# An expert kernel in which TensorE's transposes of the activation move up by one half chunk, and one VectorE subtraction moves behind two others

## The reference, cut to what matters

```
def _clamped_swiglu(hgu):
    x_glu = jnp.minimum(hgu[..., ::2], SWIGLU_LIMIT)
    x_lin = jnp.clip(hgu[..., 1::2], -SWIGLU_LIMIT, SWIGLU_LIMIT)
    return x_glu * jax.nn.sigmoid(SWIGLU_ALPHA * x_glu) * (x_lin + 1.0)
...
    xs = h[tok]
    hgu = lax.ragged_dot(xs, w_gate_up, group_sizes) + b_gate_up[e_sorted]
    act = _clamped_swiglu(hgu)
    out = lax.ragged_dot(act, w_down, group_sizes) + b_down[e_sorted]
    out = out * gates.reshape(-1)[order][:, None]
    return jax.ops.segment_sum(out, tok, num_segments=L)
```

## Time and profile before

| what | value |
|---|---|
| median of 3 runs | 1986.39 us (1986.01 to 1989.12) |
| the profiled execution's own time | 1986.01 us |
| its span, first to last instruction | 1984.3 us |
| mean granted TensorE clock | 0.984 |
| TensorE matmul busy | 1932.5 us (97%) |
| VectorE busy | 1703.8 us (86%) |
| ScalarE busy | 1372.4 us (69%) |
| GpSimd busy | 471.1 us (24%) |

### The profile page before, as it was taken

One profiled execution on the slowest core, in us unless ns is written; L12 is line 12 of the kernel. 1 busy time (PEld: TensorE's weight loads), 2 busy tenths in 40 slices (PEclk: granted clock), 3 DMA queues, 4 the chain that ended last, 5 costly groups with the idle time before them and its releaser, 6 DMA issues.

```text
span 1984.3 us, 29677 instructions
## 1 busy us (share of the span) xinstructions
PE 1932.5 (97%) x8812; PEld 1543.4 (78%) x8812; DVE 1703.8 (86%) x1759; ACT 1372.4 (69%) x1742; POOL 471.1 (24%) x339
## 2 busy tenths in 40 slices
PE   6999999998989999999999999999999999999998
PEld 3657767786768887888888888888888888888886
DVE  6899977349765479999999999999999999999998
ACT  4456855224345526888888888888888888888885
POOL 6671000000000108323222232222322223222231
PEclk7999999999999988999999999999999999999999
DMA  8222225332010256999999999999999999999995
GB/s 322 75 108 83 85 99 181 124 98 83 22 43 22 64 170 261 387 388 383 370 383 371 387 372 376 382 371 388 375 374 384 367 376 377 376 382 362 386 372 213
DMA packets 152207, 533.04 MB, mean 269 GB/s; under 512 B 14479, under 2 KB 19759, under 8 KB 149408
## 3 DMA queue, kind: packets, MB, share of 16 engines
q1 hardware_dynamic: 136112, 492.45, 65.6%
q0 software_dynamic: 16048, 39.99, 7.8%
HBM read 517.75 MB, written 24.26 MB: 273 GB/s over the span
## 4 chain that ended last, share of the span: by engine, by line
PE 89%; DVE 7%; DMA 1%; issue 1%; ACT 1%; SPq 0%; DVEq 0%; ACTq 0%
PE ps L979 55%; PE ps L1126 4%; PE ps L1174 4%; PE ps L917 3%; PE ps L1117 3%; PE ps L1155 2%; PE ps L1131 2%; PE ps L1350 2%; PE ps L1222 2%; PE ps L885 2%; PE ps L1016 2%; PE ps L856 1%; DMA arena<-in_w_down 1%; PE ps L1104 1%; PE ps L870 1%
## 5 line engine op out<-in xcount | busy, mean ns | idle before, releaser
L979 PE MATMUL ps<-split,xTs 128*128 128x512 f32 x3264 | 770.8, 392 | 0.7 <-ACT split L1798 0.5
L979 PEld LDWEIGHTS ps<-split,xTs 128*128 128x128 f32 x3264 | 610.9, 188 | 130.9 <-ACT split L1798 1.4
L2542 DVE TENSOR_TENSOR split<-arena,split 128x2048 fp32r<-128x2048 f32 x204 | 464.1, 2288 | 49.6 <-ACT split L1798 49.6
L1798 ACT ACTIVATE split<-arena 128x1024 fp32r<-128x1024 f32 x408 | 409.7, 1054 | 104.3 <-PE ps L979 103.6
L2542 DVE TENSOR_TENSOR split<-ring,split 128x2048 fp32r<-128x2048 f32 x204 | 466.0, 2317 | 0.1
L1798 ACT ACTIVATE split<-ring 128x1024 fp32r<-128x1024 f32 x408 | 410.8, 1056 | 66.6 <-PE ps L979 53.3
L979 PE MATMUL ps<-split,aTs 128*128 128x512 f32 x1632 | 386.0, 392 | 0.2 <-DVE split L2542 0.2
L979 PEld LDWEIGHTS ps<-split,aTs 128*128 128x128 f32 x1632 | 303.8, 188 | 63.2 <-DVE split L2542 0.6
L727 POOL DMA_INDIRECT arena<-h_rows,slots x33 | 91.7, 2780 | 338.5 <-PE ps L917 244.9
L775 POOL DMA_INDIRECT y_rows<-arena,slots x33 | 94.2, 2854 | 173.9 <-issue 102.3
L1960 DVE TENSOR_TENSOR split<-ring,split 128x2048 fp32r<-128x2048 f32 (+1 forms) x32 | 72.8, 2275 | 68.9 <-ACT split L1461 68.9
(11 more groups left out here) (435 smaller groups left out, 2539.3 us busy)
## 6 DMA issues: line engine op xcount, KB each, us to landing
ring<-in_w_gate_up SPq DMA_DIRECT2D x170, 1024.0 KB, 8.8
arena<-in_w_gate_up SPq DMA_DIRECT2D x102, 1024.0 KB, 7.4
arena<-in_w_down SPq DMA_DIRECT2D x102, 1024.0 KB, 10.4
ring<-in_w_down SPq DMA_DIRECT2D x34, 1024.0 KB, 10.8
ring<-in_w_in SPq DMA_DIRECT2D x23, 1024.0 KB, 5.0
ring<-in_w_out SPq DMA_DIRECT2D x8, 1024.0 KB, 5.2
ring<-in_mod_w SPq DMA_DIRECT2D x10, 512.0 KB, 9.1
ring<-in_mod_w SPq DMA_DIRECT2D x4, 1024.0 KB, 5.0
```

What stands on the lines that cost most here:

```text
L979: m = mm(ps[:, banks + q, :], lhs[:, x_, k, :], w[:, q * 512:(q + 1) * 512], start=start, stop=stop)
L1798: A(split[:, 0, c % SPLITS, :], chunk(c), ACT.Copy).then_inc(sig("hi_ready"), 1)
L2542: V.tensor_tensor(split[:, 1, s_, :].rearrange("p a b -> p (a b)"), chunk_pair(p), split[:, 0, s_, :].rearrange("p a b -> p (a b)"), ALU.s ...
```

## The change

Three orders are changed; no operation is added or taken away.

- TensorE's block of 12 transposes moves from behind the first chunk of pair 9 to ahead of pair 9 (behind pair 8), with its waits for `act_ready` and `gathered`.
- The wait for `at_lo` (low part of the second half of `aTs`) moves from the middle of chunk 20 to ahead of pair 10, in place of the wait for `at_hi` there.
- On VectorE `split_low(11)` moves behind the two `low(xTs, q)`.

```diff
                             product(c, banks, lhs, k + n_, 0, 0, start and n_ == 0, False)
-                            if p == 10 and n_ == 0:
-                                pe.wait_ge(sig("at_lo"), i * 2 + 4)
                             product(c, banks, lhs, k + n_, 1, 0, False, False).then_inc(sig("hi_used"), 1)
-                            if p == 9 and n_ == 0:
-                                turns_within()
...
-                    def turns_within():
-
-                        pe.wait_ge(sig("act_ready"), i * 2 + 2)
-                        turn(actv[:, 512:1024], 6).then_inc(sig("at_ps"), 1)
-                        pe.wait_ge(sig("gathered"), i * 16 + 32)
-                        turn(xe[:, 0:512], 7).then_inc(sig("xt_ps"), 1)
-                        turn(xe[:, 512:1024], 1).then_inc(sig("xt_ps"), 1)
...
                     for p in range(4):
                         if p == 0:
                             pe.wait_ge(sig("at_lo"), i * 2 + 3)
+                        if p == 1:
+
+                            pe.wait_ge(sig("act_ready"), i * 2 + 2)
+                            turn(actv[:, 512:1024], 6).then_inc(sig("at_ps"), 1)
+                            pe.wait_ge(sig("gathered"), i * 16 + 32)
+                            turn(xe[:, 0:512], 7).then_inc(sig("xt_ps"), 1)
+                            turn(xe[:, 512:1024], 1).then_inc(sig("xt_ps"), 1)
                         if p == 2:
-                            pe.wait_ge(sig("at_hi"), i * 2 + 2)
+                            pe.wait_ge(sig("at_lo"), i * 2 + 4)
                         pair(8 + p, 4, aTs, 2 * p, p == 0, p == 3)
...
                 split_low(10)
-                split_low(11)
                 for q in range(2):
                     dve.wait_ge(sig("xt_hi"), i * 2 + 3 + q)
                     low(xTs, q, 7 - 6 * q, sig("xt_lo"))
+                split_low(11)
```

## The result

The changed kernel takes 2003.93 us in the median of 4 runs (2002.39 to 2006.63), the kernel before 1987.34 us in the median of its 4 (1986.01 to 1989.12). The ratio is 1.0081 with a 95% interval of 1.0068 to 1.0093: 16 us slower, between 13.5 and 18.5. It is taken over all runs on record; the 16 of the changed kernel lie between 2001.69 and 2006.63 us. The two medians of 4 lie 16.6 us apart. The forecast was 2003.0 us, a loss of 16.6 us.

The account below looks back on a forecast made before the run. TensorE, never stopping in the expert loop, was taken as the bound. 33 x 0.49 + 0.4 = 16.6 us on the profiled 1986.0 gave 2002.6, plus 0.4 for the median: 2003.0 us, range 1997.5 to 2008.5.

Parts of the forecast that it names:

- TensorE sets the loop and has no wait in it: Expert loop, 34 items: TensorE busy all 35.48 us of an item, so each new wait is paid 34 times.
- The transposes wait for L2561 in every item: Block ahead of pair 9: first load 0.60 us late, plus 0.05 signal, less 0.17 regained; 0.49 us per item.
- The idle in the trace: Sign in the later profile: near 0.47 us idle beyond the usual 0.04 before the block's first load, 34 times.
- ScalarE's waits: Sign in the later profile: ScalarE waits longer for TensorE in total; no size given.
- The `at_lo` wait costs nothing: Ahead of pair 10: the moved wait is met with 1.2 us to spare, so it costs nothing.
- `split_low(11)` is met by 0.06 us: Low weights of pair 11: met because TensorE is already late; otherwise a floor of 0.32 us per item, 11 us.
- The first item: First loop item: TensorE already waits there, so the new wait costs 0.4 us instead of 0.7.
- rival A: VectorE's string before pair 11 stretches beyond 0.17 us of cover, each 0.1 us costing 3.4 us; 2005.5 to 2010; chance 0.15.
- the case that nothing is regained: At the transposes' wait: the late start costs in full, 0.65 us per item, 22 us in all, 2008.5 us.
- B (overtaking): TensorE runs chunk 18's ready matmuls while the transposes wait: not slower, 1986.4 us; chance 0.03.
- C (the clock): New gaps lower TensorE's clock to 1.2 GHz; the loop's 1206 us grows by as much again if throughout; chance 0.01.
- D (gaps relieved): Stream after the transposes: slack removed by the new order, 0.03 us per item, 1 us; no chance of its own.

Follow-up runs that it names:

- both waits cured: The full change with the eight `xe` transposes ahead of the activation's four and VectorE's order as before: 35.48 us an item, 1987.71 us against 1988.2 for the kernel before.

## Why the prediction was right, point by point

**TensorE sets the loop and has no wait in it.** Shown: four matmuls less per item are 30 us less time, and every late start of TensorE came out as time, less what it regains. With both waits cured nothing was gained over before.

**The transposes wait for L2561 in every item.** Forecast 0.49 us an item, measured 0.49, and the block alone gives the full loss. The runs at two and eight matmuls up give the line of which this is one point, and its offset, the 0.17 us regained. The forecast took this regain from one transpose elsewhere in the trace; that it holds in the loop is shown.

**The idle in the trace.** Here the prediction's text was wrong: it said that the block's first load would show near 0.47 us of idle beyond the usual 0.04. The row shows 0.69, so 0.65 beyond. The idle of a load is its lateness, 0.60 + 0.05, before anything is regained; I had written the cost (near 0.49) where the lateness belongs. The sum did not use that number.

**ScalarE's waits.** Here the text was wrong too: ScalarE was to wait longer for TensorE in total. Its chunks wait less for TensorE, 138.5 us instead of 143.4. What grew is their wait for `split_low`, 31.5 us; before it was

```profile
ACT split L1798 <- DVE split L2542: 9.1, 31, 0.3
```

With the transposes alone moved it is as forecast, 171.1 us for TensorE. With the full change `split_low(11)` frees the slot of the next item's chunk 2 later, and one such wait of 1.04 us stands in the timeline above. The prediction had named this delay and held it to be hidden from TensorE; it is, the 36 loads and those behind them show no idle.

**The `at_lo` wait costs nothing.** Measured alone: 35.48 us. The wait for `gathered` costs nothing either: no row of TensorE names it in the full change.

**`split_low(11)` is met by 0.06 us, only because TensorE is late already.** Measured: met by 0.03 us in the full change; alone the order costs 0.34 us an item (forecast 0.32). That the two do not add was shown by doing each alone.

**The first item.** Forecast 0.4 us, measured 0.95. This term was mis-sized. The waits of before were swallowed, as forecast (0.57 us, and the small ones that follow it). But two things came in their place: the transposes' load stood idle 1.47 us instead of 0.69, and a new wait of 0.57 us came at the low weights of pair 11:

```profile
781.24 1.06 ACT L1793 ACTIVATE split<-arena 128x1024 fp32r<-128x1024 f32 x1 [2.29 <-DMA arena<-in_w_down]
...
785.14 1.29 PEld L917 LDWEIGHTS ps<-const,arena 128*128 128x128 f32 x12 [1.47 <-issue]
...
785.23 2.01 ACT L1793 ACTIVATE split<-arena 128x1024 fp32r<-128x1024 f32 x2 [0.64 <-DMA arena<-in_w_down]
...
787.76 0.69 DVE L2441 TENSOR_TENSOR aTs<-ps,aTs 128x512 fp32r<-128x512 f32 x1 [0.47 <-ACT aTs L1767]
...
794.10 0.76 PEld L979 LDWEIGHTS ps<-split,aTs 128*128 128x128 f32 x4 [0.57 <-DVE split L2537]
```

The trace names no releaser for the first wait, but L2556 ends at 785.09, 0.05 us ahead of the load. The activation came late behind a chunk that waited for its DMA (781.24). The next chunks waited for DMA as well (785.23), ScalarE's copy to `aTs` came behind them, and VectorE stood 0.47 us for it. So VectorE needs 9.64 us from the start of L2556 (784.40) to the end of `split_low(11)` (794.04), where in the later item above it needs 9.10 (1216.49 to 1225.59). The 0.54 us more are the lateness of pair 11. This is what rival A described, in this one item.

How much of the 0.95 us is the change and how much the landing of those tiles stays open. The first item lasts 36.66 us with the `at_lo` wait alone and 36.09 with both waits cured, kernels whose later items are those of before. It lasts 36.57 with the transposes alone, 35.88 with them two matmuls up and 37.57 with VectorE's order alone, in no proportion to what the later items lose. The same holds for the 0.81 us ahead of the first item's transposes, where no instruction was changed; over the other runs that stretch ends between 1.2 us sooner and 2.3 us later than in the kernel before.

**How much of the hit is luck.** What was worked out and then measured is the 0.49 us per item. That the total came within 1 us is partly luck: the first item alone missed by 0.55 us, the stretch ahead of it moved by 0.81, and single runs of the changed kernel lie 5 us apart. The chances given for the kinds of slower outcome also add up to 0.95, not to the 0.94 stated.

**The rivals.** A (the second wait adds): outside the first item it did not, by 0.03 us, and the case that nothing is regained is out by the run at two matmuls up. B (overtaking): no; then the three distances would have shown no loss. C (the clock): the granted clock is 1.00 in the loop, with 0.27 us in each item without a matmul. D (gaps relieved): with both waits cured the item is 35.48 us, not shorter.

## What to carry to other kernels

Where an engine has no wait in a loop, ask of every reordering how early each of its waits is met today; here 0.30 us of cover stood against a move of 0.91 us, and the difference, less the little that a late start regains, is paid in every item. Look for the second wait that the first one hides: its price alone is what remains when the first is cured. What has its data already (here the eight transposes of `xe`) goes ahead of what still waits. The move was then free here, though on an engine that never idled it gained nothing either.

## What the runs showed of the hardware that was not expected

A weight load that starts late costs less than its lateness, and what comes back hardly depends on how late it is. For a transpose 0.20 us late cost 0.03, 0.65 cost 0.49 and 1.56 cost 1.39, so 0.16 to 0.17 us came back each time; the prediction had this from one case, the three are new. For a 512-column matmul 0.43 us cost 0.34, so 0.09 came back. The idle that the profile shows ahead of such a load is here the lateness and the stream's own 0.04 us, not the loss; the loss is read from the distance between the same instruction in two items.
